# Gates of tokens 128 to 255 by indirect transfer in all expert blocks, and lo of U's second half made in two instructions

## The chip, the cores and the metric
One core of a Trainium2 chip runs the whole layer. The metric is the device time of one execution in microseconds. Before the change it was 1037.93 us, the median of three (1037.75 to 1038.24).

## What is computed
A decoder block on 256 tokens of width 1024 in float32: a token mixer (two kinds of attention, gated) and then PEER, a layer with 16384 experts. The change concerns PEER alone:

```python
def chunk_fn(xc):
    q = (xc @ wq).reshape(PEER_CHUNK, PEER_HEADS, 2, PEER_QDIM // 2)
    sc = jnp.einsum('thpd,pkd->thpk', q, subkeys)
    sv, si = lax.top_k(sc, PEER_TOPK)
    cand = sv[:, :, 0, :, None] + sv[:, :, 1, None, :]
    cv, ci = lax.top_k(cand.reshape(PEER_CHUNK, PEER_HEADS, PEER_TOPK * PEER_TOPK), PEER_TOPK)
    i1 = jnp.take_along_axis(si[:, :, 0], ci // PEER_TOPK, axis=-1)
    i2 = jnp.take_along_axis(si[:, :, 1], ci % PEER_TOPK, axis=-1)
    e = i1 * PEER_NKEYS + i2
    g = jax.nn.softmax(cv.astype(jnp.float32), axis=-1)
    act = jax.nn.gelu(jnp.einsum('td,thkd->thk', xc, u[e]))
    return jnp.einsum('thk,thkd->td', g * act, v[e])
```

Each token picks 16 experts in each of 8 heads. The kernel does not gather them: it computes gelu(x u) for all 128 blocks of 128 experts, multiplies it by a gate that is the softmax weight where an expert was picked and zero elsewhere, and multiplies by all of v.

## The kernel before
Weights come from HBM in tiles of 128x1024 through a ring of four (`raw`). Each is split so that TensorE's products are accurate: ScalarE copies it to a rounded `hi` (`loop_hi`, L1200), VectorE subtracts to get `lo` (`loop_lo`, L1676); both have three slots. TensorE then adds hi x hi, hi x lo and lo x hi.

After the token mixer (to about 270 us) come 128 **tiles of U** (`u_tile`, L831 to L833: 24 matmuls of 256 columns), whose gelu fills `big`, one block of 256 tokens per tile. Then come 128 **tiles of V** (`v_tile`, L889: 12 matmuls of 512 columns), whose stationary operands are the gated blocks, split as well: `auxh` by ScalarE (`w_hi`, L1227) and `auxl` by VectorE (`w_lo`, L1856), in three slots. TensorE's order is fixed: tile after tile.

**The router** (the choice of experts) runs beside the first 62 tiles of U: VectorE finds the best keys (`choose_keys`), GpSimd adds pairs of scores, VectorE finds the best pairs, GpSimd multiplies by key numbers and VectorE sums them, with one exponential on ScalarE. VectorE's code places `loop_lo` between these by hand: `spread(n)` makes lo of all tiles up to n+2. Head numbers 0 to 7 are those of tokens 0 to 127 and 8 to 15 those of tokens 128 to 255.

**Gates come in two ways.** A *group* (`g_group`, L844) serves four tokens and 64 blocks: ScalarE makes a one-hot `oneB` (four squares, L1215, and a Relu, L1221), VectorE a comparison `same` (L1795) and `oneA` (L1803), TensorE four matmuls of 128 columns, VectorE a reduction `gsum` (`add_parts`, L1811) and the product into `big` (`weigh`, L1818). There are 96: 64 for all tokens in blocks 0 to 63, one to a tile in U's second half, and 32 for tokens 0 to 127 in blocks 64 to 127, one to two tiles in V's first half. The gates of tokens 128 to 255 in blocks 64 to 127 are *scattered*: 128 indirect DMAs from GpSimd (L1992) add weights into the cleared `gate_d` in HBM, each sixteenth waiting for the ones before; SP brings them back as blocks of 128x128 (`gring`, four slots), and VectorE multiplies (`gate_block`, L1870), announcing each by the semaphore `gated`. That happens in V's second half.

Every engine runs its queue in order, so what stands behind a wait waits too. What sets the order around the change in V's first and second half are these lines of ScalarE's queue before:

```python
def v_step_g(i, j):
    if j % 2 == 0:
        squares_b(i, NGRP + 2 + j // 2, UNROLL // 2)
    w_hi(i, j + SPLIT - 1)
    if j % 2:
        relu_b(i, NGRP + 2 + j // 2, UNROLL // 2)
    loop_hi(i, V0 + j + SPLIT)
def v_step_gated(i, j):
    loop_hi(i, V0 + HALF + j + SPLIT)
    w_hi_gated(i, j + SPLIT)
```

Of the kernel before, what the change touches and what calls it, by code (L numbers as in the profile page):

```python
# [30 lines left out]
P = 128  # L31
D = 1024
T = 256
# [31 lines left out]
NGRP = T // 4  # L65
NGRP_V = P // 4
# [3 lines left out]
TILES_KEYS, TILES_PAIRS = 14, 25  # L70
TILES_NUMBERS = ROUTER - 2 - TILES_KEYS - TILES_PAIRS
# [20 lines left out]
def build(nc, x_d, wpre_d, u_d, v_d, par_d, cst_d, kep_d, out_d):  # L92
    with ExitStack() as ctx:
# [20 lines left out]
        eT = sb("eT", [P, 3, T])  # L114
# [187 lines left out]
        def _(sp):  # L302
# [40 lines left out]
            stream(v_d, N_PRE + NBLK, 0, HALF)  # L343
# [4 lines left out]
            sp.wait_ge(scattered, 16 * 16 * NH)  # L348

            def v_and_gates(i, j):  # L350

                sp.wait_ge(lo_done, i * UNROLL + splits(N_PRE + NBLK + HALF + GRING + j - RING + 1))
                load(splits(N_PRE + NBLK + HALF + GRING + j) % RING,
                     v_d[bass.ds(i * UNROLL + (HALF + GRING + j), 1)].rearrange("a p c -> (a p) c"))
                sp.wait_ge(S("gated"), i * UNROLL + (j + 1))
                sp.dma_start(gring[:, j % GRING, :], gate_tiles[bass.ds(i * UNROLL + (HALF + GRING + j), 1)].rearrange(
                    "a p t -> (a p) t")).then_inc(gate_in[j % GRING], 16)

            for m in range(GRING):
                sp.dma_start(gring[:, m, :], gate_tiles[HALF + m]).then_inc(gate_in[m], 16)  # L360
            for m in range(GRING):
                sp.wait_ge(lo_done, splits(N_PRE + NBLK + HALF + m - RING + 1))
                load(splits(N_PRE + NBLK + HALF + m) % RING, v_d[HALF + m])
            each_tile(sp, HALF - GRING, v_and_gates)
# [7 lines left out]
        def _(pe):  # L372
# [482 lines left out]
            for w, src in enumerate((i1f, i2f)):  # L855
                for b in range(TB):
                    m = pe.transpose(bank[6][:, w * T + b * P:w * T + (b + 1) * P], src[:, b * P:(b + 1) * P], ident)
            m.then_inc(S("keysT"), 1)
            pe.wait_ge(S("router"), 1)
            for b in range(TB):  # L860
                m = pe.transpose(bank[7][:, b * P:(b + 1) * P], chosen_w[:, b * P:(b + 1) * P], ident)
            m.then_inc(S("routerT"), 1)
# [4 lines left out]
            def g_and_u(i, j):  # L867
                g_group(i, j, UNROLL)
                u_tile(i, j, HALF)

            each_tile(pe, NGRP, g_and_u)
            g_group(0, NGRP, UNROLL)
# [35 lines left out]
            def g_and_v(i, j):  # L908
                if j % 2 == 0:
                    g_group(i, NGRP + 1 + j // 2, UNROLL // 2)  # L910
                v_tile(i, j, 1)

            v_tile(0, 0, 0, first=True, parts=1)
            each_tile(pe, 2 * NGRP_V - 4, g_and_v)
            g_group(0, NGRP + NGRP_V - 1, UNROLL // 2)
            each_tile(pe, NBLK - 3 - (2 * NGRP_V - 4), lambda i, j: v_tile(i, j, 1 + 2 * NGRP_V - 4))
# [4 lines left out]
        def _(act):  # L921
# [307 lines left out]

            def w_hi_tokens(b, tb, done):  # L1230
# [17 lines left out]
            each_tile(act, ROUTER - 2, u_step)  # L1248
            act.preload_act_table_set(LN_EXP)
            act.wait_ge(S("router_d"), 1)  # L1250
            for b in range(TB):
                of_b = gwt[:, b * P:(b + 1) * P]
                m = act.activation(of_b, of_b, ACT.Exp, scale=rs2[:, b:b + 1])
            m.then_inc(S("router_exp"), 1)
            act.preload_act_table_set(GELU)
# [15 lines left out]
            relu_b(0, NGRP, UNROLL)
            act.wait_ge(S("weighed"), 1 + NGRP)
            w_hi_tokens(0, 1, "whi_done")
            for b in range(1, SPLIT - 1):
                w_hi(0, b)
            squares_b(0, NGRP + 1, UNROLL)
            relu_b(0, NGRP + 1, UNROLL)
# [4 lines left out]
            def v_step_g(i, j):  # L1282
                if j % 2 == 0:
                    squares_b(i, NGRP + 2 + j // 2, UNROLL // 2)
                w_hi(i, j + SPLIT - 1)
                if j % 2:
                    relu_b(i, NGRP + 2 + j // 2, UNROLL // 2)
                loop_hi(i, V0 + j + SPLIT)

            def w_hi_gated(i, m):  # L1290
                act.wait_ge(S("gated"), i * UNROLL + (m + 1))
                w_hi(i, HALF + m)
# [5 lines left out]
            each_tile(act, 2 * NGRP_V - 4, v_step_g)  # L1298
            w_hi(0, HALF - 2)
# [815 lines left out]
```

## Time and profile before
| what | us |
|---|---|
| median of three | 1037.93 |
| the profiled execution | 1038.22 |
| its span, first to last instruction | 1036.3 |
| TensorE busy | 1028.7 |
| VectorE busy | 846.6 |
| ScalarE busy | 677.7 |
| GpSimd busy | 337.7 |
| U's tiles | 269 to 668 |
| V's tiles | 669 to 1033 |

Names in a row are output<-inputs. A row of a timeline gives the start in us from the span's start, the duration, engine, line, operation, and in brackets the engine's idle time before it and who ended it. Consecutive instructions overlap in the records (a start comes before the end of the one before), so the cost of one in a full queue is the distance between starts, not its duration.

### The profile page before, as it was taken

What the parts mean: (1) busy time and instruction counts of PE and PEld (TensorE: products, weight loads), DVE (VectorE), ACT (ScalarE), POOL (GpSimd) and SP (SyncE); (2) the same over time, 40 slices, a digit from 0 to 9 for tenths busy, and PEclk for the clock granted to TensorE, in tenths of its full rate; (3) what the DMA queues carried; (4) which work ended last, traced back from release to release, by engine and by line L of the source; (5) the groups of instructions that cost most, each with busy time, mean ns of one, the idle gap of its engine ahead of it and who ended that gap; (6) DMA issues with size and microseconds to landing.
All of it is one profiled execution on the core that took longest, in us unless ns stands there. A gap on an engine that the chain in (4) does not pass through costs nothing.

```text
span 1036.3 us, 21770 instructions
## 1 busy us (share of the span) xinstructions
PE 1028.7 (99%) x6945; PEld 936.3 (90%) x6945; DVE 846.6 (82%) x1673; ACT 677.7 (65%) x1283; POOL 337.7 (33%) x227
## 2 busy tenths in 40 slices
PE   8999999999999999999999999999999999999998
PEld 7798889999999999999999999988888888888887
DVE  6767886788999879999999999998888876666665
ACT  5456776665544444488988889877777764545453
POOL 0010321008102117667867688777700000000000
PEclk9999999999999999999999999999999999999999
DMA  8664555655455555566666666677755566666663
GB/s 340 250 224 154 188 181 183 196 187 187 154 191 182 180 186 182 182 171 157 161 162 157 152 158 161 143 184 183 174 174 179 182 232 207 210 222 212 220 214 123
DMA packets 80256, 194.01 MB, mean 187 GB/s; under 512 B 25296, under 2 KB 33616, under 8 KB 80208
## 3 DMA queue, kind: packets, MB, share of 16 engines
q1 hardware_dynamic: 59328, 184.79, 53.7%
q0 software_dynamic: 20736, 8.46, 7.3%
q8 instruction: 26, 0.43, 0.2%
q10 hardware_dynamic: 144, 0.14, 0.1%
q14 instruction: 22, 0.18, 0.1%
HBM read 182.81 MB, written 10.55 MB: 187 GB/s over the span
## 4 chain that ended last, share of the span: by engine, by line
PE 98%; DVE 0%; DMA 0%; ACT 0%; issue 0%; ACTq 0%; DVEq 0%
PE bank L889 33%; PE bank L831 12%; PE bank L833 12%; PE bank L832 12%; PE bank L844 4%; PE bank L385 2%; PE bank L386 2%; PE bank L387 2%; PE bank L451 2%; PE bank L771 2%; PE bank L455 1%; PE bank L467 1%; PE bank L468 1%; PE bank L469 1%; PE bank L748 1%; PE bank L749 1%
## 5 line engine op out<-in xcount | busy, mean ns | idle before, releaser
L1200 ACT ACTIVATE hi<-raw 128x1024 fp32r<-128x1024 f32 x253 | 268.2, 1060 | 248.5 <-PE bank L889 132.3
L1676 DVE TENSOR_TENSOR lo<-raw,hi 128x1024 fp32r<-128x1024 f32 x253 | 318.5, 1259 | 106.5 <-ACT hi L1200 106.2
L831 PE MATMUL bank<-xhi,hi 128*128 128x256 f32 x1024 | 292.9, 286 | 0.0
L833 PE MATMUL bank<-xhi,lo 128*128 128x256 f32 x1024 | 290.0, 283 | 0.0
L832 PE MATMUL bank<-xlo,hi 128*128 128x256 f32 x1024 | 289.7, 283 | 0.0
L1992 POOL DMA_INDIRECT gate_d<-chosen_w,chosen_at x128 | 234.9, 1835 | 72.3 <-issue 48.3
L831 PEld LDWEIGHTS bank<-xhi,hi 128*128 128x128 f32 x1024 | 196.6, 192 | 0.0
L832 PEld LDWEIGHTS bank<-xlo,hi 128*128 128x128 f32 x1024 | 196.3, 192 | 0.0
L833 PEld LDWEIGHTS bank<-xhi,lo 128*128 128x128 f32 x1024 | 196.1, 191 | 0.0
L889 PE MATMUL bank<-hi,auxh 128*128 128x512 f32 x504 | 157.4, 393 | 1.0 <-DVE auxl L1863 0.9
L889 PE MATMUL bank<-hi,auxl 128*128 128x512 f32 x504 | 155.6, 390 | 0.0
L889 PE MATMUL bank<-lo,auxh 128*128 128x512 f32 x504 | 155.5, 390 | 0.0
L1215 ACT ACTIVATE oneB<-kep,eT 128x128 fp32r<-128x128 f32 x384 | 121.5, 388 | 0.0
L889 PEld LDWEIGHTS bank<-hi,auxl 128*128 128x128 f32 x504 | 94.6, 188 | 20.0
L889 PEld LDWEIGHTS bank<-lo,auxh 128*128 128x128 f32 x504 | 94.6, 188 | 20.0
L1324 DVE TENSOR_TENSOR lo<-raw,hi 128x1024 fp32r<-128x1024 f32 x73 | 90.1, 1243 | 26.1 <-ACT hi L934 25.7
L889 PEld LDWEIGHTS bank<-hi,auxh 128*128 128x128 f32 x504 | 92.2, 188 | 18.9 <-issue 1.0
L934 ACT ACTIVATE hi<-raw 128x1024 fp32r<-128x1024 f32 x73 | 77.1, 1058 | 45.9 <-PE bank L455 19.2
L1811 DVE TENSOR_REDUCE gsum<-bank 128x256 f32<-128x512 f32 x96 | 65.8, 686 | 1.7 <-PE bank L844 0.5
L1803 DVE TENSOR_TENSOR oneA<-same,gw 128x512 fp32r<-128x512 f32 x96 | 65.7, 685 | 0.0
L1856 DVE TENSOR_TENSOR auxl<-big,auxh 128x256 fp32r<-128x256 f32 x127 | 53.3, 420 | 9.7 <-ACT auxh L1227 9.7
L1221 ACT ACTIVATE oneB<-oneB 128x512 fp32r<-128x512 f32 x96 | 59.1, 616 | 0.1
(393 smaller groups left out, 1559.6 us busy)
## 6 DMA issues: line engine op xcount, KB each, us to landing
raw<-u_d SPq DMA_DIRECT2D x128, 512.0 KB, 3.3
raw<-v_d SPq DMA_DIRECT2D x128, 512.0 KB, 3.3
raw<-wpre_d SPq DMA_DIRECT2D x70, 512.0 KB, 4.3
gate_d<-big POOLq DMA_DIRECT2D x16, 512.0 KB, 5.2
big<-wpre_d SPq DMA_DIRECT2D x8, 512.0 KB, 7.9
gring<-gate_d SPq DMA_DIRECT2D x64, 64.0 KB, 2.9
gate_d<-chosen_w,chosen_at POOLq DMA_INDIRECT x128
big<-x_d SPq DMA_DIRECT2D x4, 256.0 KB, 4.2
```

Source lines behind the costliest of these rows:

```text
L831: pe.matmul(out, wh, xhi[:, k, :], start=(k == 0), stop=False)
L832: pe.matmul(out, wh, xlo[:, k, :], start=False, stop=False)
L833: m = pe.matmul(out, wl, xhi[:, k, :], start=False, stop=(k == KT - 1))
L889: m = pe.matmul(bank[2 * b + f][:, :], a_, w_[:, s, f * 512:(f + 1) * 512], start=(first and st_ == 0), stop=False, skip_group_check=True)
L934: act.activation(hi[:, slot(n), :], raw[:, splits(n) % RING, :], ACT.Copy).then_inc(hi_done, 1)
L1200: act.activation(hi[:, slot(n), :], raw[:, splits(n) % RING, :], ACT.Copy).then_inc(hi_done, 1)
L1215: m = act.activation(oneB[:, g % 2, t, :], iota, ACT.Square, bias=i2, scale=-1.0)
L1324: dve.tensor_tensor(lo[:, slot(n), :], raw[:, splits(n) % RING, :], hi[:, slot(n), :].bitcast(F32), ALU.subtract).then_inc(lo_done, 1)
L1676: dve.tensor_tensor(lo[:, slot(n), :], raw[:, splits(n) % RING, :], hi[:, slot(n), :].bitcast(F32), ALU.subtract).then_inc(lo_done, 1)
L1803: dve.tensor_tensor(oneA[:, g % 2, :, :, :], eq_, w_.unsqueeze(3).broadcast_to([P, 4, 2, HALF]), ALU.mult).then_inc(S("oneA_ready"), 1)
L1811: dve.tensor_reduce(gsum[:, :, :], parts, AXX, ALU.add).then_inc(S("bank67_read"), 1)
L1992: pool.indirect_dma_start(gate_d, bass.IndirectOffsetOnAxis(chosen_at[:, c:c + 1], 0), chosen_w[:, P + c:P + c + 1], None, compute_op=ALU. ...
```

## The change
1. Groups serve tokens 0 to 127 only: 32 for blocks 0 to 63, one to two tiles of U's second half, and the same 32 as before in V's first half. The scattered gates now serve tokens 128 to 255 in all 128 blocks; the number of indirect DMAs stays 128.
2. Their data are needed from V's first block on. So the router treats the heads of tokens 128 to 255 first, in three pieces (heads 8 and 9, 10 to 15, then 0 to 7), with three exponentials, and GpSimd issues scatters between the sums and picks, 42 of them before the last numbers are picked.
3. In V, SP loads 128 gate blocks, VectorE multiplies each right behind lo, and ScalarE's `w_hi` waits for it.
4. In U's second half VectorE makes lo in two instructions of 512 columns.
5. SP brings `h` back behind 60 of V's steps.

```diff
-NGRP = T // 4
-NGRP_V = P // 4
+NGRP = P // 4
+GT = UNROLL // 2
+EXP_AT = (8, 20, 51)
```

SP:

```diff
-            stream(v_d, N_PRE + NBLK, 0, HALF)
+            for m in range(GRING):
+                sp.wait_ge(lo_done, splits(N_PRE + NBLK + m - RING + 1))
+                load(splits(N_PRE + NBLK + m) % RING, v_d[m])
+            sp.wait_ge(scattered, 16 * 16 * NH)
+            for m in range(GRING):
+                sp.dma_start(gring[:, m, :], gate_tiles[m]).then_inc(gate_in[m], 16)
+            def v_and_gates(i, j):
+                sp.wait_ge(lo_done, i * UNROLL + splits(N_PRE + NBLK + GRING + j - RING + 1))
+                load(splits(N_PRE + NBLK + GRING + j) % RING,
+                     v_d[bass.ds(i * UNROLL + (GRING + j), 1)].rearrange("a p c -> (a p) c"))
+                sp.wait_ge(S("gated"), i * UNROLL + (j + 1))
+                sp.dma_start(gring[:, j % GRING, :], gate_tiles[bass.ds(i * UNROLL + (GRING + j), 1)].rearrange(
+                    "a p t -> (a p) t")).then_inc(gate_in[j % GRING], 16)
+            each_tile(sp, HALF - GRING, v_and_gates)
```

TensorE, U's second half:

```diff
-                g_group(i, j, UNROLL)
+                if j % 2 == 0:
+                    g_group(i, j // 2, GT)
                 u_tile(i, j, HALF)
```

ScalarE:

```diff
+            def weights_exp(z, b, c0, c1):
+                act.preload_act_table_set(LN_EXP)
+                act.wait_ge(S("router_d"), z + 1)
+                of_heads = gwt[:, c0 * 16:c1 * 16]
+                act.activation(of_heads, of_heads, ACT.Exp, scale=rs2[:, b:b + 1]).then_inc(S("router_exp"), 1)
+                act.preload_act_table_set(GELU)
+            u_steps(0, EXP_AT[0])
+            weights_exp(0, 1, NH, NH + 2)
+            u_steps(EXP_AT[0], EXP_AT[1])
+            weights_exp(1, 1, NH + 2, 2 * NH)
...
+            act.wait_ge(S("weighed"), 1 + NGRP)
             w_hi_tokens(0, 0, "whi_tokens")
+            act.wait_ge(S("gated"), 1)
             w_hi_tokens(0, 1, "whi_done")
+            w_hi_gated(0, 1)
...
             def v_step_g(i, j):
                 if j % 2 == 0:
+                    squares_b(i, NGRP + 2 + j // 2, GT)
-                w_hi(i, j + SPLIT - 1)
+                w_hi_gated(i, j + SPLIT - 1)
                 if j % 2:
+                    relu_b(i, NGRP + 2 + j // 2, GT)
                 loop_hi(i, V0 + j + SPLIT)
-            def v_step_gated(i, j):
-                loop_hi(i, V0 + HALF + j + SPLIT)
-                w_hi_gated(i, j + SPLIT)
+            def v_step(i, j):
+                w_hi_gated(i, HALF + j)
+                loop_hi(i, V0 + HALF + j + 1)
```

VectorE:

```diff
+            numbers(NH, NH + 2, 6, 9)
+            weights(0, NH, NH + 2)
+            dve.wait_ge(S("cleared"), 16 * 16)
+            addresses(NH, NH + 2)
+            for z in range(3):
+                choose_pairs(NH + 2 + 2 * z, 12 + 3 * z)
+            from_best(NH + 2, 2 * NH)
+            numbers(NH + 2, 2 * NH, 18, 26)
...
+            def loop_lo_halves(i, n):
+                dve.wait_ge(hi_done, i * UNROLL + splits(n + 1))
+                dve.tensor_tensor(lo[:, slot(n), 0:512], raw[:, splits(n) % RING, 0:512],
+                                  hi[:, slot(n), 0:512].bitcast(F32), ALU.subtract).then_inc(S("lo_first"), 1)
+                dve.tensor_tensor(lo[:, slot(n), 512:1024], raw[:, splits(n) % RING, 512:1024],
+                                  hi[:, slot(n), 512:1024].bitcast(F32), ALU.subtract).then_inc(lo_done, 1)
...
+            w_lo_tokens(0, 0, "whi_tokens", 1, "wlo_tokens")
+            add_parts(0, NGRP, GT)
+            keys_equal(0, NGRP + 3, GT)
+            gate_block(0, 0)
+            gate_block(0, 1)
+            w_lo_tokens(0, 1, "whi_done", 1, "wlo_done")
+            gate_block(0, 2)
+            w_lo(0, 1)
...
+            def v_step(i, j):
+                w_lo(i, j + SPLIT - 1)
+                loop_lo(i, V0 + j + SPLIT)
+                gate_block(i, j + SPLIT)
             def v_step_g(i, j, keys=True, rows=True):
...
                 loop_lo(i, V0 + j + SPLIT)
+                gate_block(i, j + SPLIT)
```

The order of the instructions shows three places. ScalarE, one odd step of the loop over V's first half (`auxh` is w_hi, `oneB` the Relu, ISA computes an address), before:

```order
L1227 ISA
L1227 ACTIVATE auxh<-big 128x256
L1220 REGISTER_ALU
L1221 ACTIVATE oneB<-oneB 128x512 [waits dist_sq]
L1199 REGISTER_ALU [waits tile_loaded2]
L1200 ACTIVATE hi<-raw 128x1024 [waits tile_used]
```

and now:

```order
L1229 REGISTER_ALU
L1224 ISA [waits gated]
L1224 ACTIVATE auxh<-big 128x256
L1217 REGISTER_ALU
L1218 ACTIVATE oneB<-oneB 128x512 [waits dist_sq]
L1196 REGISTER_ALU [waits tile_loaded2]
L1197 ACTIVATE hi<-raw 128x1024 [waits tile_used]
```

The copy to `auxh` has got a wait for `gated`, on the register operation ahead of it, and hi stands behind both.

VectorE, the same loop (`auxl` is w_lo, `oneA` the group's operand), an odd step, before:

```order
L1856 ISA [waits whi_done]
L1856 TENSOR_TENSOR auxl<-big,auxh 128x256
L1816 REGISTER_ALU
L1818 ISA [waits bank67_read]
L1818 TENSOR_TENSOR big<-gsum,big 128x64x4
L1803 ISA [waits same]
L1803 TENSOR_TENSOR oneA<-same,gw 128x512
L1675 REGISTER_ALU
L1676 TENSOR_TENSOR lo<-raw,hi 128x1024 [waits hi_done]
```

and now:

```order
L1916 ISA [waits whi_done]
L1916 TENSOR_TENSOR auxl<-big,auxh 128x256
L1865 REGISTER_ALU
L1867 ISA [waits bank67_read]
L1867 TENSOR_TENSOR big<-gsum,big 128x64x4
L1852 ISA [waits same]
L1852 TENSOR_TENSOR oneA<-same,gw 128x512
L1681 REGISTER_ALU
L1682 TENSOR_TENSOR lo<-raw,hi 128x1024 [waits hi_done]
L1928 REGISTER_ALU
L1930 ISA [waits gate_in0]
L1930 TENSOR_TENSOR big<-big,gring 128x128
```

The product with `gring`, which announces `gated`, stands last in the step, behind lo.

GpSimd, the router and the scatters (L2026 sums of pairs, L2036 picks), before:

```order
L1975 TENSOR_TENSOR big<-big 128x256 [waits keys_chosen]
L1975 TENSOR_TENSOR big<-big 128x256 x3
L1975 TENSOR_TENSOR big<-big 128x256 [waits pairs_chosen] x12
L1983 TENSOR_TENSOR big<-big 128x256 [waits placed] x32
L1992 DMA gate_d<-chosen_w,chosen_at 2097152x1 [waits chosen,router]
L1992 DMA gate_d<-chosen_w,chosen_at 2097152x1 x15
L1992 DMA gate_d<-chosen_w,chosen_at 2097152x1 [waits scattered]
```

and now:

```order
L2036 TENSOR_TENSOR big<-big 128x256 [waits placed] x4
L2046 DMA gate_d<-chosen_w,chosen_at 2097152x1 [waits chosen,router,keys_chosen]
L2046 DMA gate_d<-chosen_w,chosen_at 2097152x1 x2
L2026 TENSOR_TENSOR big<-big 128x256 [waits pairs_chosen] x2
L2046 DMA gate_d<-chosen_w,chosen_at 2097152x1 x8
L2036 TENSOR_TENSOR big<-big 128x256 [waits placed] x4
L2046 DMA gate_d<-chosen_w,chosen_at 2097152x1
L2036 TENSOR_TENSOR big<-big 128x256 [waits placed] x4
L2046 DMA gate_d<-chosen_w,chosen_at 2097152x1
L2036 TENSOR_TENSOR big<-big 128x256 [waits placed] x4
L2046 DMA gate_d<-chosen_w,chosen_at 2097152x1
L2046 DMA gate_d<-chosen_w,chosen_at 2097152x1 [waits chosen,router]
```

The scatters have moved from behind all sums and picks to between them; the list goes on in this manner.

## Rows read from the trace of the kernel before
**Rows 1.** The page: span, and busy time, share and instructions of each engine (part 1).
```profile
span 1036.3 us, 21770 instructions
...
PE 1028.7 (99%) x6945; PEld 936.3 (90%) x6945; DVE 846.6 (82%) x1673; ACT 677.7 (65%) x1283; POOL 337.7 (33%) x227
```

**Rows 2.** The chain of waits in time: start us, us, what.
```profile
491.96 0.39 PE bank L844 x4
...
495.29 0.39 PE bank L844 x4
...
708.18 5.53 PE bank L889 x24
...
714.11 5.53 PE bank L889 x24
...
858.75 168.96 PE bank L889 x744
...
1027.70 5.45 PE bank L904 x24
```

**Rows 3.** Timeline of ScalarE in U's first half: start us, us, instruction [idle before].
```profile
437.36 1.06 ACT L1200 ACTIVATE hi<-raw 128x1024 fp32r<-128x1024 f32 x1 [1.82 <-PE bank L833]
...
440.24 1.06 ACT L1200 ACTIVATE hi<-raw 128x1024 fp32r<-128x1024 f32 x1 [1.34 <-PE bank L833]
```

**Rows 4.** Timeline of TensorE between tiles 61 and 62 of U: the transposes.
```profile
448.69 0.60 PE L857 MATMUL bank<-kep,big 128*128 128x128 f32 x4
```

**Rows 5.** Timeline of VectorE in V's first half.
```profile
737.41 0.42 DVE L1856 TENSOR_TENSOR auxl<-big,auxh 128x256 fp32r<-128x256 f32 x1 [0.36 <-ACT auxh L1227]
737.85 0.69 DVE L1811 TENSOR_REDUCE gsum<-bank 128x256 f32<-128x512 f32 x1
738.46 0.42 DVE L1795 TENSOR_TENSOR same<-kep,eT 128x256 f32<-128x256 f32 x1
738.79 1.22 DVE L1676 TENSOR_TENSOR lo<-raw,hi 128x1024 fp32r<-128x1024 f32 x1
```

**Rows 6.** Timeline of ScalarE and VectorE in V's second half.
```profile
899.90 1.06 ACT L1200 ACTIVATE hi<-raw 128x1024 fp32r<-128x1024 f32 x1 [1.35 <-PE bank L889]
...
901.00 1.23 DVE L1676 TENSOR_TENSOR lo<-raw,hi 128x1024 fp32r<-128x1024 f32 x1 [0.95 <-ACT hi L1200]
902.14 0.28 DVE L1870 TENSOR_TENSOR big<-big,gring 128x128 f32 x1
```

**Rows 7.** Timeline of both late in V's first half, VectorE's addresses constant.
```profile
831.69 0.40 ACT L1227 ACTIVATE auxh<-big 128x256 fp32r x1
...
832.13 0.43 DVE L1856 TENSOR_TENSOR auxl<-big,auxh 128x256 fp32r<-128x256 f32 x1 [0.25 <-ACT auxh L1227]
```

**Rows 8.** Timeline of ScalarE at the step of rows 5.
```profile
736.87 0.40 ACT L1227 ACTIVATE auxh<-big 128x256 fp32r x1
...
738.42 0.40 ACT L1227 ACTIVATE auxh<-big 128x256 fp32r x1
738.73 0.62 ACT L1221 ACTIVATE oneB<-oneB 128x512 fp32r<-128x512 f32 x1
```

**Rows 9.** Timeline of ScalarE and VectorE in U's first half: the router.
```profile
444.69 1.28 ACT L1249 ACT_TABLE_LOAD   x1
...
445.36 1.39 DVE L1756 TENSOR_REDUCE big<-big 128x16 f32<-128x256 f32 x4
...
313.47 0.75 DVE L1690 MAX8 big<-big 128x8 f32<-128x256 f32 x2
...
316.36 1.21 DVE L1676 TENSOR_TENSOR lo<-raw,hi 128x1024 fp32r<-128x1024 f32 x1
```

**Rows 10.** Instructions on gate_d (ns min/median/max, first and last start), timelines of GpSimd and VectorE.
```profile
L1992 POOL DMA_INDIRECT gate_d<-chosen_w,chosen_at x128: 1553/1572/3488, 450.5 to 749.5; - x128
...
542.95 2.60 POOL L1992 DMA_INDIRECT gate_d<-chosen_w,chosen_at  x1 [0.30 <-issue]
...
542.89 1.22 DVE L1676 TENSOR_TENSOR lo<-raw,hi 128x1024 fp32r<-128x1024 f32 x1 [0.23 <-ACT hi L1200]
```

More of the change, by code:

```diff
@@ L347, in _ @@
                 sp.dma_start(h[:, b, :], out_d[b * P:(b + 1) * P, :]).then_inc(S("h_back"), 16)
[L348 to L364, printed above, removed]
+            each_tile(sp, HALF, lambda i, j: v_and_gates(i, HALF - GRING + j))
             for z, (b, c, w) in enumerate(out_parts_v):
@@ L855, in _ @@
             for w, src in enumerate((i1f, i2f)):
-                for b in range(TB):
-                    m = pe.transpose(bank[6][:, w * T + b * P:w * T + (b + 1) * P], src[:, b * P:(b + 1) * P], ident)
+                m = pe.transpose(bank[6][:, w * P:(w + 1) * P], src[:, 0:P], ident)
             m.then_inc(S("keysT"), 1)
[L859 to L862, printed above, removed]
+            pe.wait_ge(S("router"), 3)
+            pe.transpose(bank[7][:, 0:P], chosen_w[:, 0:P], ident).then_inc(S("routerT"), 1)
             for j in range(ROUTER, HALF):
@@ L1228, in w_hi, with w_hi_gated @@
                                ACT.Copy).then_inc(S("whi_done"), 1)
+            def w_hi_gated(i, b):
+                act.wait_ge(S("gated"), i * UNROLL + (b + 1))
+                w_hi(i, b)
             def w_hi_tokens(b, tb, done):
@@ new lines, in weights, with addresses @@
+            def weights(z, c0, c1):
+                sums, ones = smx[:, c0:c1], smx[:, 16 + c0:16 + c1]
+                dve.wait_ge(S("router_exp"), z + 1)
+                link(dve.tensor_reduce(sums, g3[:, c0:c1], AXX, ALU.add))
+                link(dve.reciprocal(ones, sums))
+                dve.tensor_tensor(w3[:, c0:c1], g3[:, c0:c1], ones.unsqueeze(2).broadcast_to([P, c1 - c0, 16]),
+                                  ALU.mult).then_inc(S("router"), 1)
+            def addresses(c0, c1):
+                of_heads = slice(c0 * 16, c1 * 16)
+                link(dve.scalar_tensor_tensor(caf[:, of_heads], i1f[:, of_heads], 128.0, i2f[:, of_heads], ALU.mult, ALU.add))
+                dve.tensor_scalar(chosen_at[:, c0 * 16 - P:c1 * 16 - P], caf[:, of_heads], float(P), tok_at,
+                                  ALU.mult, ALU.add).then_inc(S("chosen"), 1)
@@ L1782, in _ @@
+            from_best(NH + 2, 2 * NH)
+            numbers(NH + 2, 2 * NH, 18, 26)
+            weights(1, NH + 2, 2 * NH)
+            addresses(NH + 2, 2 * NH)
+            for c in range(1, NH):
+                choose_keys(c)
+                spread(26 + (11 * c) // 7)
+            keys_ready()
+            for z in range(4):
+                choose_pairs(2 * z, 40 + 3 * z)
+            from_best(0, NH)
+            numbers(0, NH, 49, ROUTER - 2)
+            weights(2, 0, NH)
             dve.wait_ge(S("keysT"), 1)
-            dve.tensor_copy(eT[:, 0:2, :], bank[6][:, :].rearrange("p (w t) -> p w t", w=2)).then_inc(S("bank67_read"), 1)
+            dve.tensor_copy(eT[:, 0:2, :], bank[6][:, 0:2 * P].rearrange("p (w t) -> p w t", w=2)).then_inc(S("bank67_read"), 1)
@@ L1976, in _, with pick @@
                                    ALU.add).then_inc(S("pair_sums"), 1)
-            for c in range(16):
+            def pick(c):
+                q = (c - NH) % (2 * NH)
                 for side in range(2):
-                    pool.wait_ge(S("placed"), 2 * c + side + 1)
+                    pool.wait_ge(S("placed"), 2 * q + side + 1)
                     e3 = eqt[c % 2][side].rearrange("p (k a) -> p k a", k=16)
```

305 lines of the change are left out of this document (155 added, 150 removed).

## The prediction
> **What bounds the kernel now.** I read the page first, then the chain of waits, then the timeline of single engines. The span is 1036.3 us and TensorE is busy for 99% of it, VectorE 82%, ScalarE 65% [rows 1]; the granted clock is full in every stretch. The chain that ended last is TensorE from end to end in both large stages [rows 2]. Its pieces give the prices. In U's second half a group of gate matmuls plus a tile of U takes 495.29 - 491.96 = 3.33, of which a tile alone is 2.88, the spacing of ScalarE's hi instructions in U's first half [rows 3]; so a group costs 0.44 there. In V's first half two blocks and a group take 714.11 - 708.18 = 5.93. In V's second half 62 blocks take 168.96, 2.725 each. The last two blocks take 5.45. So whatever takes a group from TensorE is worth its time, as long as ScalarE and VectorE still deliver one block's four operands (hi, lo of V; auxh, auxl of the gated activations) every 2.965 us in V's first half and every 2.725 in its second.
>
> **Removed.** 32 of 96 groups, all in U's second half: 32 x 0.44 = -14.1 us. Three of six transposes, at most 0.60 / 4 each [rows 4]: -0.4. The squares, Relus, comparisons and reductions of 32 groups leave ScalarE and VectorE too, which are not on the path there, so nothing more comes off.
>
> **Lo in halves.** Two instructions of 512 columns at a spacing of 0.61 [rows 5] (738.46 - 737.85) take 1.22 where one takes 1.14 (902.14 - 901.00) [rows 6]: +0.08 each on VectorE, 63 times. Two tiles of U and a group now last 2 x 2.88 + 0.44 = 6.2 us, in which VectorE has 4 x 0.61 of lo and four group instructions (0.61, 0.33, 0.33, 0.61): 4.3. Hidden by 1.9 us of idle time; without that cover it would be 5 us.
>
> **V: a wait that closes a ring.** This is the term that decides. In step j of V's first half ScalarE now does w_hi of block j+2 behind the wait for `gated` (block j+2), and hi of V's tile j+3 stands behind it in ScalarE's queue. The gating of block j+2 is VectorE's last instruction of step j-1, behind lo of tile j+2, which waits for ScalarE's hi of tile j+2. So hi(n), lo(n), gate(n), w_hi(n), hi(n+1) are one chain, each the start of the next, with no slack to gain on. Before, tokens 128 to 255 of the first half needed no gating, and in the second half gates ran ahead (four in the ring, gate j+3 done behind lo of j+2), so that the same chain spanned two blocks. One turn, from rows:
> - hi start to lo start: 901.00 - 899.90 = 1.10 [rows 6];
> - lo to gate: 1.14; the gate lasts 0.28 [rows 6];
> - gate end to w_hi start: 0.04 where the address is a constant (831.69 + 0.40 to 832.13) [rows 7], 0.14 where it is computed from the loop's register (736.87 + 0.40 to 737.41) [rows 5, 8]. Those rows are VectorE's behind ScalarE; the new wait stands on the register operation itself, as there, so I take 0.14, with 0.04 as the other end;
> - w_hi to the next start on ScalarE: 0.31 (738.73 - 738.42) [rows 8].
>
> Sum 2.97, taken as 2.96, against TensorE's 2.725: V's second half loses 63 x 0.235 = **+14.8**. With the constant's 0.04 it would be 2.86 and +8.5.
>
> In V's first half more stands in the ring. Even steps (the four squares stand ahead of the wait and are done before it ends): after w_hi (0.40 + 0.14) VectorE does auxl (0.33), the reduction (0.61), the comparison (0.33) and then lo (1.14), gate (0.28), 0.14: 3.37. (A start follows an instruction of 0.41 after 0.33 [rows 5].) Odd steps: w_hi 0.31, Relu 0.62 less the 0.09 by which its follower starts early, hi to lo 1.10, then 1.14 + 0.28 + 0.14: 3.50. A pair is 6.84 with rounding against TensorE's 5.93. 28 pairs: **+25.5**. Six last steps have less in them: +1.2. At the start TensorE has about 1.1 us in hand (estimate: auxl of block 2 is due that long before its tile): -1.1. At the end the last two blocks are interleaved; auxl of block 127 comes 2.96 after that of 126 where TensorE needs 5.45 / 8 = 0.68 between them: +2.3. The passage from U to V itself: the halves of block 0 now wait for the last weighing and for the first gate; nearly as long as before (-0.4). The ring in all: **+42.3**; with 0.04 for all latencies of 0.14 some 150 of them give back 0.1 each, +27.
>
> **U's first half.** The router is now done in three pieces, and VectorE waits for GpSimd where that has scatters in its queue ahead of sums and picks. GpSimd's 128 indirect transfers move from behind everything to between these: 42 are in U's first half, and all 16-packs wait for completion. Tile 12 is the place that I can price. Tiles start at 448.69 - 2.88 x (62 - j), tile 12 at 304.7. ScalarE does hi of tile 11 only behind the exponential and two table loads of 1.28 [rows 9]: some 1.6 late, so lo of tile 11 ends at 300.1. Before lo of tile 12 VectorE has four picks' sums (1.39) [rows 9], five small instructions for weights and addresses (estimate 1.6), and eight instructions on pairs (316.36 - 313.47 = 2.9) [rows 9]: lo starts at 306.0 and ends 1.2 later, 2.5 us late. Three more joints with GpSimd (the numbers of heads 10 to 15, the first pair sums of tokens 0 to 127, the last numbers) come out within 2 us of their due time; I give them 1 us together. **+3.5**, between 0 and 9.
>
> **Scatters.** 86 are left when the last numbers are picked, near 453. Before, their spacing was (749.5 - 450.5) / 127 = 2.35 [rows 10], waits for a pack among it. At that pace they start until 453 + 85 x 2.35 = 653, land some 4.5 later, and the gates' loads (2.9 to landing, 0.4 to issue) would be in at 661, where block 0 wants its gate at about 658. So cover ends just there. But a scatter that starts just behind a lo of 1024 columns takes 2.60 in place of the median 1.57 [rows 10], 1.03 more; with 512 columns less is to be waited for. The sum takes 2.2, done before 650, cost 0; ends are 0 and +6. The Trainium skill says in SBUF — State Buffer, "SBUF: two separate sides", that VectorE with two SBUF inputs and a reading GpSimd hold a shared pair for a whole instruction, whoever starts first. By that rule a half holds it for about half as long, and the scatters are in time; the row of 2.60 agrees, while no run here shows the halves.
>
> SP's queue has the loads of V's tiles 0 to 3 ahead of the wait for `scattered`, and each gate load behind its V load: the ring gives each over 11 us for 2.9. The reload of h (moved behind 60 blocks) has 180 us. Both nothing.
>
> **Sum.** -14.1 - 0.4 + 42.3 + 3.5 = +31.3, on the profiled span of 1036.3: 1067.6. That execution took 1038.22, 1.92 above its span, and 0.29 above the median of 1037.93. So 1069.2, say **1069**.
>
> **Rivals.**
> - The ring turns at constant-address latency (0.04) everywhere: +27 - 14.5 + 3.5 = +16, 1054; without a slip in U 1050. For: ScalarE's register operation may be shorter than VectorE's. Against: the one row of a computed address behind a wait. 18%.
> - The scatters are late: +6 more, 1075, if their spacing stays at 2.35. Against: halves and a less busy VectorE. 10%.
> - Faster, the other side: the ring does not bind and TensorE keeps its 2.725 and 5.93. Then only -14.5 and the slip count: 1023 to 1027. It needs mean turns under 2.93 us where 2.96 and 3.43 come out of rows (mean 3.2), each link being one that another pair of engines must wait for. The order of the instructions leaves no way around it; it decides from a mean of 0.08 us per block up (10 us over 125 blocks). 8%: 5 of them clearly faster, 2 within the noise, 1 slower.
> - The change does less than it says: no; the groups are gone from TensorE's order, 14.1 us at 0.44.
>
> The main case has 64%. Faster by over 0.2% (what a measurement here can tell from no change) 0.05, within it 0.02, slower 0.93. Range: 1050 (no late address, no slip) to 1080 (slip of 9, late scatters).
>
> **What would show it.** In V's second half hi's spacing should be 2.96 (2.86 in the rival), with ScalarE idle before w_hi until VectorE's gate, not before hi until TensorE; VectorE idle until ScalarE's hi; TensorE idle in each block by 0.2, waiting for auxl. In V's first half pairs of 6.84. In U's second half groups every 6.2. A first gate load before 652. I am wrong if hi in V still waits for TensorE.

## The result and the profile after

The change is slower: 1070.74 us, the median of four (1070.33 to 1072.60), against 1038.09 (1037.75 to 1038.68) before; ratio 1.0317, 95% interval 1.0300 to 1.0335. The forecast was 1069, in a range of 1050 to 1080. The profiled execution took 1070.51 us with a span of 1068.7, where the prediction's sum gave 1067.6. One of gate_first's four executions below took 1419.68 us at a mean granted clock of 0.655; it is left out of every number.

The page of the kernel after: span, busy times, and the shares of the chain that ended last, by engine and by line.

```profile
span 1068.7 us, 21198 instructions
...
PE 1046.5 (98%) x6814; PEld 913.6 (85%) x6814; DVE 817.6 (76%) x1694; ACT 629.7 (59%) x1128; POOL 327.6 (31%) x227
...
PE 57%; DVE 15%; issue 14%; ACT 11%; DVEq 1%; ACTq 1%; DMA 0%; SPq 0%
```

The engines' busy shares hardly differ from [rows 1], and "PE 98%" would let one take TensorE for the bound still. The chain says otherwise: only 57% of it is TensorE's, where it was 98% before. TensorE's busy time has even grown by 18 us with 131 instructions fewer. The ends of matmuls are modelled, and in V one that is followed by a short pause counts as longer (the hi x auxh matmuls last 414 ns in the mean where they lasted 393 before). So the chain and the idle times decide here, not the busy share. Idle time by who ended it, in the kernel after (engine, output, line; who was waited for; us in total, times, longest):

```profile
ACT auxh L1224 <- DVE big L1930: 175.5, 125, 2.0
DVE auxl L1916 <- ACT auxh L1224: 83.8, 126, 0.7
PEld bank L886 <- DVE auxl L1916: 33.4, 87, 0.5
PE bank L830 <- DVE lo L1682: 2.8, 3, 1.9
PE bank L901 <- DVE auxl L1916: 1.9, 1, 1.9
```

ScalarE waits 125 times in V for the gate product (L1930), and no longer once before hi for TensorE, as it did in [rows 6]. TensorE's weight loads wait for auxl: it is now the engine that is fed late.

**The ring in V's second half.** Timelines of ScalarE and VectorE, kernel after (start us, us, instruction, idle before it):

```profile
952.20 1.04 ACT L1197 ACTIVATE hi<-raw 128x1024 fp32r<-128x1024 f32 x1
954.82 0.42 ACT L1224 ACTIVATE auxh<-big 128x256 fp32r x1 [1.58 <-DVE big L1930]
955.15 1.04 ACT L1197 ACTIVATE hi<-raw 128x1024 fp32r<-128x1024 f32 x1
```

```profile
953.27 1.23 DVE L1682 TENSOR_TENSOR lo<-raw,hi 128x1024 fp32r<-128x1024 f32 x1 [0.41 <-ACT hi L1197]
954.41 0.28 DVE L1930 TENSOR_TENSOR big<-big,gring 128x128 f32 x1
```

One can follow the turn: hi at 952.20, lo 1.07 later, the gate 1.14 behind lo, auxh 0.41 behind the gate's start (0.28 of it, then 0.13 until ScalarE goes on), the next hi 0.33 later: 2.95 from hi to hi. TensorE needs 2.725 for a block [rows 2].

**The ring in V's first half**, VectorE in the kernel after. Two steps last from lo to lo 732.32 - 725.46 = 6.86, where TensorE could do them in 5.93:

```profile
725.46 1.22 DVE L1682 TENSOR_TENSOR lo<-raw,hi 128x1024 fp32r<-128x1024 f32 x1
726.59 0.28 DVE L1930 TENSOR_TENSOR big<-big,gring 128x128 f32 x1
727.56 0.42 DVE L1916 TENSOR_TENSOR auxl<-big,auxh 128x256 fp32r<-128x256 f32 x1 [0.68 <-ACT auxh L1224]
...
732.32 1.22 DVE L1682 TENSOR_TENSOR lo<-raw,hi 128x1024 fp32r<-128x1024 f32 x1
```

**U's first half.** TensorE's matmul that opens tile 12 (timeline, kernel after), and VectorE's piece before it:

```profile
306.81 0.36 PE L830 MATMUL bank<-xhi,hi 128*128 128x256 f32 x1 [1.89 <-DVE lo L1682]
...
356.49 0.35 PE L830 MATMUL bank<-xhi,hi 128*128 128x256 f32 x1 [0.49 <-DVE lo L1682]
359.96 0.36 PE L830 MATMUL bank<-xhi,hi 128*128 128x256 f32 x1 [0.37 <-DVE lo L1682]
```

```profile
299.09 1.22 DVE L1682 TENSOR_TENSOR lo<-raw,hi 128x1024 fp32r<-128x1024 f32 x1 [2.18 <-ACT hi L1197]
300.23 1.39 DVE L1760 TENSOR_REDUCE big<-big 128x16 f32<-128x256 f32 x4
...
305.45 2.35 DVE L1682 TENSOR_TENSOR lo<-raw,hi 128x1024 fp32r<-128x1024 f32 x2
```

Between the lo of tile 11 at 299.09 and that of tile 12 at 305.45 lie 6.4 us, in which TensorE has work for 2.88. The transposes that were at 448.69 [rows 4] are at 452.19: a slip of 3.5. In this trace V's first group of gate matmuls starts at 656.67, where the kernel before had it at 667.76.

**Scatters and gate loads**, all transfers on gate_d of the kernel after from 449 to 647 us (ns min/median/max, first and last start), and SP's first four loads of gates:

```profile
L2046 POOL DMA_INDIRECT gate_d<-chosen_w,chosen_at x87: 1561/1640/2387, 448.9 to 646.6; - x87
```

```profile
L347 SPq DMA_DIRECT2D gring<-gate_d x4: 328/432/433, 651.4 to 652.7; - x4
```

Their spacing is (646.6 - 448.9) / 86 = 2.30. The last one starts at 646.6, the loads leave from 651.4, and block 0 of V begins at 657.7 after 0.5 us of waiting: in time.

**The tail.** The chain's last entries, and windows of the kernel after (window, length, then busy time of PE, PEld, DVE, ACT, POOL with instructions, the granted clock of TensorE, DMA share, GB/s):

```profile
1056.41 1.23 DVE lo L1682
1058.89 6.67 PE bank L901 x21
```

```profile
1057.00:1060.00 3.00, 1.11 (x5) 0.97 (x6) 1.33 (x4) 0.42 (x1) 0.00 (x0) 1.00 0.02 5
1060.00:1064.00 4.00, 4.00 (x13) 3.09 (x12) 1.31 (x2) 0.00 (x0) 0.00 (x0) 0.57 0.28 105
1064.00:1068.00 4.00, 1.54 (x7) 0.94 (x5) 1.37 (x2) 0.00 (x0) 0.00 (x0) 1.00 0.42 159
```

21 matmuls take 6.67 us where before 24 took 5.45 [rows 2]. TensorE had stood for 1.9 us; from 1060.1 to 1063.8 nine matmuls then start 0.41 apart on average in place of 0.23, at a granted clock of 0.57 of full speed, that is mostly at the lower level of 1.2 GHz. That costs 1.6 us which no step of the prediction had.

### The profile page after: what moved, and what is told of

Same layout as the page of the kernel before. It is cut to its first block, busy times and chain, and to the rows that moved or that the text cites. A ratio compares the mean times of both kernels' runs of the same rounds, so it can differ in the third digit from the quotient of the medians.

```text
span 1068.7 us, 21198 instructions
## 1 busy us (share of the span) xinstructions
PE 1046.5 (98%) x6814; PEld 913.6 (85%) x6814; DVE 817.6 (76%) x1694; ACT 629.7 (59%) x1128; POOL 327.6 (31%) x227
## 4 chain that ended last, share of the span: by engine, by line
PE 57%; DVE 15%; issue 14%; ACT 11%; DVEq 1%; ACTq 1%; DMA 0%; SPq 0%
PE bank L830 10%; PE bank L832 10%; PE bank L831 10%; ACT hi L1197 8%; DVE lo L1682 6%; DVE big L1930 3%; ACT auxh L1224 3%; PE bank L384 2%; PE bank L385 2%; PE bank L386 2%; PE bank L450 2%; PE bank L770 2%; DVE gsum L1860 2%; DVE oneA L1852 2%; PE bank L454 1%
## 5 line engine op out<-in xcount | busy, mean ns | idle before, releaser
L830 PE MATMUL bank<-xhi,hi 128*128 128x256 f32 x1024 | 291.7, 285 | 2.8 <-DVE lo L1682 2.8
L1682 DVE TENSOR_TENSOR lo<-raw,hi 128x1024 fp32r<-128x1024 f32 x190 | 242.4, 1280 | 38.3 <-ACT hi L1197 37.6
L2046 POOL DMA_INDIRECT gate_d<-chosen_w,chosen_at x128 | 231.3, 1807 | 74.0 <-issue 48.1
L886 PE MATMUL bank<-hi,auxh 128*128 128x512 f32 x504 | 168.0, 414 | 1.8 <-DVE auxl L1923 0.5
L1224 ACT ACTIVATE auxh<-big 128x256 fp32r (+1 forms) x127 | 53.1, 418 | 175.5 <-DVE big L1930 175.5
L886 PEld LDWEIGHTS bank<-hi,auxh 128*128 128x128 f32 x504 | 85.1, 188 | 46.7 <-DVE auxl L1916 33.4
L1330 DVE TENSOR_TENSOR lo<-raw,hi 128x1024 fp32r<-128x1024 f32 x73 | 90.1, 1244 | 26.1 <-ACT hi L931 25.9
L1889 DVE TENSOR_TENSOR lo<-raw,hi 128x512 fp32r<-128x512 f32 x63 | 43.6, 693 | 54.9 <-ACT hi L1197 54.9
L1212 ACT ACTIVATE oneB<-kep,eT 128x128 fp32r<-128x128 f32 x256 | 81.1, 389 | 0.0
L384 PE MATMUL bank<-xhi,hi 128*128 128x256 f32 x192 | 56.2, 293 | 0.0
```

The source lines that it names most:

```text
L384: pe.matmul(out, wh, xh, start=(k == 0), stop=False)
L830: pe.matmul(out, wh, xhi[:, k, :], start=(k == 0), stop=False)
L886: m = pe.matmul(bank[2 * b + f][:, :], a_, w_[:, s, f * 512:(f + 1) * 512], start=(first and st_ == 0), stop=False, skip_group_check=True)
L1212: m = act.activation(oneB[:, g % 2, t, :], iota, ACT.Square, bias=i2, scale=-1.0)
L1224: act.activation(auxh[:, s * T:(s + 1) * T], big[:, bass.ds(i * (UNROLL * T) + b * T, T)], ACT.Copy).then_inc(S("whi_done"), 1)
L1330: dve.tensor_tensor(lo[:, slot(n), :], raw[:, splits(n) % RING, :], hi[:, slot(n), :].bitcast(F32), ALU.subtract).then_inc(lo_done, 1)
```

## The experiments

The theory: the gate product behind lo closes a ring of ScalarE and VectorE, and that is worth +42.3; the rest of the change is worth -14.5 and +3.5. The main rivals: the loss comes from the added work or transfers in V, or from the scatters. All ratios are against the kernel before, run on the same chip (its medians were 1038.07 to 1038.46). The sizes of single parts below are read from the profiled executions; V is counted from its first group of gate matmuls on.

**gate_first.** The product stands ahead of lo, in both of VectorE's loops in V. The same instructions, in another order:

```diff
                 w_lo(i, j + SPLIT - 1)
-                loop_lo(i, V0 + j + SPLIT)
                 gate_block(i, j + SPLIT)
+                loop_lo(i, V0 + j + SPLIT)
...
-                loop_lo(i, V0 + j + SPLIT)
                 gate_block(i, j + SPLIT)
+                loop_lo(i, V0 + j + SPLIT)
```

> In both V steps the gating of block j+3 is moved ahead of lo of tile j+3 on VectorE; the instructions and their number stay. Ring theory: hi, lo, gate, w_hi no longer follow each other in one turn; what is left of it (w_hi, auxl, group work, gate) is 0.54 + 0.33 + 0.94 + 0.28 + 0.14 = 2.2 us, under TensorE's 2.965 and 2.725. So pairs of 5.93 in V's first half, 2.725 a block in its second, and about 43 us off 1070.7: 1027 to 1029, hi in V waiting for TensorE again. Rival, VectorE or the gate loads simply have too much to do in V (128 gatings and loads in place of 64): the order changes nothing, 1068 to 1072.

Measured: 1026.80 us, the median of three (1026.79, 1026.80, 1029.31), ratio 0.990 (0.988 to 0.992); the profiled execution took 1026.80, span 1025.0. So 43.7 us hang on the place of an instruction of 0.28 us, 1.6 of them through the clock in the tail. The chain of this kernel in V is TensorE's again:

```profile
839.51 176.88 PE bank L886 x780
1016.39 5.45 PE bank L901 x24
```

and ScalarE in V's second half waits for TensorE before hi, with 2.71 between them:

```profile
899.47 1.06 ACT L1197 ACTIVATE hi<-raw 128x1024 fp32r<-128x1024 f32 x1 [1.35 <-PE bank L886]
...
902.18 1.06 ACT L1197 ACTIVATE hi<-raw 128x1024 fp32r<-128x1024 f32 x1 [1.35 <-PE bank L886]
```

All of the added products, gate loads and waits are still there. They cost nothing off the ring.

**ring_dose.** V's lo in halves as well, with the change's order: a dose of some 0.07 us in a link of the ring, and on VectorE.

```diff
 in v_step and v_step_g:
-                loop_lo(i, V0 + j + SPLIT)
+                loop_lo_halves(i, V0 + j + SPLIT)
```

> As the change, but lo of V is made in two instructions of 512 columns too, which puts the gate 1.20 to 1.22 us behind lo's start in place of 1.14. Ring theory: each of some 125 turns is 0.06 to 0.08 longer, 1070.7 + 7.5 to 10 = 1078 to 1081; spacing of hi in V's second half 3.01 to 3.03 in place of 2.95. If the wait were for something outside this ring (gate loads, TensorE), nothing: 1070 to 1072.

Measured: 1079.61 (two executions), ratio 1.0397 (1.0376 to 1.0417), 8.9 above the change. VectorE in V's second half, where lo starts 3.03 apart:

```profile
949.31 0.69 DVE L1889 TENSOR_TENSOR lo<-raw,hi 128x512 fp32r<-128x512 f32 x1 [0.41 <-ACT hi L1197]
...
950.52 0.28 DVE L1930 TENSOR_TENSOR big<-big,gring 128x128 f32 x1
...
952.34 0.69 DVE L1889 TENSOR_TENSOR lo<-raw,hi 128x512 fp32r<-128x512 f32 x1 [0.40 <-ACT hi L1197]
```

The two traces also differ by the clock, and not only by the dose. This one has a stretch at the lower clock in U (0.72 and 0.71 from 306 to 312, against 1.00 in the change), and V's first group starts at 658.83, 2.2 later; its tail has the full clock, 1.6 less (21 matmuls in 5.06 us). From V's first group to these 21 matmuls it is 1069.41 - 658.83 = 410.6 us here and 1058.89 - 656.67 = 402.2 in the change: the dose itself costs 8.4, 0.07 for each of some 125 blocks.

**gate_first_dose.** Both edits together: the same dose, off the ring.

> The gate ahead of lo, and V's lo in halves. Ring theory: lo is in no ring, VectorE has 5.2 + 0.14 of 5.93 us in a pair, so the same as with the gate first alone, 1027 to 1030. If VectorE's load is the bound, 7 to 10 us more than with the gate first alone.

Measured: 1027.68 (1026.51 and 1028.84), ratio 0.9897 (0.9877 to 0.9916). V takes 1024.7 - 656.6 = 368.1 us of its trace, and 1025.0 - 656.9 = 368.1 of gate_first's. The same work that costs 8.4 us in the ring costs nothing outside of it. VectorE's load is no bound.

**gate_first_v2.** The order is changed in V's second half alone (`v_step`), which splits the ring's price.

> The gate ahead of lo only in the steps of V's second half; the first half keeps the change's order. Ring theory, by its two terms: 63 x (2.95 - 2.725) = 14 and the tail's 2 come back, the first half's 26 to 27 stay: 1070.7 - 16 = 1054 to 1055.5, with pairs of 6.86 in the first half and 2.725 in the second.

Measured: 1052.87 (1052.55 and 1053.18), ratio 1.0139 (1.0119 to 1.0159), about 1 below the expectation. The span of the profiled execution is 1051.4, 17.3 below that of the change. Its tail, at the full clock and without the wait, has the length of before again:

```profile
873.85 168.93 PE bank L886 x744
1042.78 5.46 PE bank L901 x24
```

The tail begins at 1042.78 and V's first group at 657.30, against 1056.03 and 656.67 in the change. So the 63 turns of the second half are worth (1056.03 - 656.67) - (1042.78 - 657.30) = 13.9, and were priced at 14.8. The tail is worth 4.0 more, 2.1 of wait and 1.6 of clock among it; the expectation had 2 for it, since I had not counted the clock, and so lay too high. What remains above gate_first is the first half's: V takes 394.1 us here and 368.1 there, 26.0, priced at 25.5 + 1.2 - 1.1 = 25.6 (the -0.4 of the passage from U to V is in both kernels). The pairs of the first half last 6.86 here too.

**ring_const.** ScalarE's loop over V's second half is written out, so that the operation behind `gated` has a constant address. Nothing else changes.

```diff
-            each_tile(act, HALF - 1, v_step)
+            for j in range(HALF - 1):
+                v_step(0, j)
```

> The change with ScalarE's loop over V's second half written out, so that w_hi's address is a constant; VectorE and the order stay. If the wait on a register operation costs 0.08 to 0.10 more than one on the copy itself, hi's spacing in the second half falls from 2.95 to 2.85 to 2.87: 60 x 0.08 to 0.10 = 5 to 6 less, 1064.5 to 1066. If the latency has nothing to do with the address: 1070 to 1071.

Measured: 1065.47 (1063.28 and 1067.66), ratio 1.026 (1.0233 to 1.0288). The median lies in the expected range only because it is the mean of two times outside it, 4.4 apart, so the trace has to decide. ScalarE in this kernel:

```profile
952.31 1.04 ACT L1197 ACTIVATE hi<-raw 128x1024 fp32r<-128x1024 f32 x1
954.85 0.42 ACT L1224 ACTIVATE auxh<-big 128x256 fp32r<-128x256 f32 x1 [1.49 <-DVE big L1931]
955.17 1.04 ACT L1197 ACTIVATE hi<-raw 128x1024 fp32r<-128x1024 f32 x1
```

The turn is 2.86 in place of 2.95, and the wait 1.49 in place of 1.58: the computed address costs 0.09 behind a wait. 63 x 0.09 = 5.7. The 21 last matmuls start at 1053.12, 5.8 earlier than in the change. The rest of the profiled execution's gain (1070.51 - 1063.28 = 7.2) is the clock: it is full in the tail of this trace. The execution of 1067.66 has a mean clock of 0.998 where the traced one has 1.000; where it lost its 4.4 us, no trace shows.

**lo_whole.** The change, with lo of U's second half in one instruction again.

```diff
-                    loop_lo_halves(i, N_PRE + HALF + j + SPLIT)
+                    loop_lo(i, N_PRE + HALF + j + SPLIT)
```

> As the change, but lo of U's second half is one instruction of 1024 columns again. My term for the scatters: their spacing goes back from 2.30 to about 2.38 with durations of 2.6 among them, the last starts near 653.6 in place of 646.6, and block 0's gate comes about 3 us late (the loads' issue and landing behind it): 1073 to 1075. If halves matter for nothing else than that and the cover is longer than I think: 1070 to 1071.

Measured: 1073.29 (1073.19, 1073.39), ratio 1.0336 (1.0315 to 1.0356). It met the expectation of scatters that come 2.5 us late, for another reason. Its last scatter does start late, at 653.3, but VectorE's first gate product (661.25) stands right behind the comparison before it, with no idle time, and from V's first group (659.55) to the 21 last matmuls (1061.59) it is 402.0 us, as in the change. The loss is in U: the transposes between tiles 61 and 62 are already at 454.82, 2.6 us behind those of the change, and up to there the two kernels have the same instructions. The next runs separate the two.

**gate_first_whole.** gate_first with the same edit, **gate_first_again** the same file as gate_first, both on one chip.

> The gate first, lo of U's second half whole. Scatters' term: with the ring gone the late first gate still costs the 2.5 us that it cost with the ring in place (1073.3 against 1070.7), since TensorE is the bound behind it: 1029 to 1030 against 1026.8. If V had room to catch up, less: 1027 to 1028.

> The gate first once more, beside the other two: 1026.5 to 1028.

Measured: whole 1027.68 (1026.47 to 1029.60), ratio 0.9903 (0.9886 to 0.9920); again 1028.89 (1026.47 to 1029.29), ratio 0.9903 (0.9886 to 0.9919). Again lies above its expected range, and the expected cost of a whole lo is not there, although its last scatter starts 3.5 us later than gate_first's 646.9:

```profile
L2046 POOL DMA_INDIRECT gate_d<-chosen_w,chosen_at x128: 1548/1641/3698, 303.3 to 650.4; - x128
```

Both spread over the same two values. The windows behind the stall at tile 12, gate_first_again (span 1027.0) and then gate_first_whole (span 1024.7), columns as above:

```profile
306.00:309.00 3.00, 2.47 (x15) 2.50 (x16) 3.00 (x7) 0.27 (x1) 2.96 (x1) 0.72 0.40 149
309.00:312.00 3.00, 3.00 (x20) 3.00 (x20) 3.00 (x13) 0.77 (x1) 2.74 (x3) 0.71 0.97 284
```

```profile
306.00:309.00 3.00, 2.46 (x20) 2.49 (x21) 3.00 (x7) 0.29 (x1) 2.97 (x1) 1.00 0.48 171
309.00:312.00 3.00, 3.00 (x27) 3.00 (x26) 3.00 (x13) 1.06 (x1) 2.73 (x3) 1.00 0.96 257
```

Both had the stall of 1.9 us (1.90 and 1.89); one of them ran some 3.4 us at the lower clock behind it. lo_whole's trace has that stretch as well, at 0.74 and 0.69 in the same windows, and the profiled execution of the change at 1.00 in both. That is lo_whole's +2.6 (its second execution, 1073.39, has the same mean clock, 0.997, but no trace).

**before_halves.** The kernel before, with lo in halves in U's second half.

> The kernel before with lo of U's second half in two instructions and nothing else. VectorE has 0.23 us of idle time in 3.32 and gets 0.06 to 0.08 more to do: the same time, 1037.5 to 1038.7. The scatters that meet this stretch (86 of 128) get closer, 2.30 or less in place of 2.38, with no durations of 2.6 among them, without effect on the time. If the fixed cost of an instruction were larger than I take it, U's steps would be longer than 3.32 and the time up by some us.

Measured: 1038.25 (ten executions, 1037.73 to 1038.90), ratio 1.000 (0.999 to 1.0009). The halves cost TensorE nothing, even with a group per tile. The scatters in its trace end at 731.1 in place of 749.5 [rows 10], and of those that start until 655 none takes over 2.23 us, where 20 of the kernel before take over 2.5.

**gate_first_spreads.** gate_first, with lo of the next tiles placed earlier in VectorE's router, at the two joints where TensorE had waited.

```diff
             weights(0, NH, NH + 2)
+            spread(10)
...
             weights(1, NH + 2, 2 * NH)
+            spread(27)
             addresses(NH + 2, 2 * NH)
```

> The gate ahead of lo, and lo of one more tile placed right behind the weights of heads 8 and 9 (before their addresses and the next pairs) and behind those of heads 10 to 15. The stalls of 1.9, 0.5 and 0.4 us that the change's trace has in U's first half are for lo behind that work, so all go if the place is the cause: 2.8 less than the gate first alone, 1024 to 1026. If GpSimd's lateness is the cause, the stalls move to the next tile and the time stays at 1027 to 1028.

Measured: 1025.57 (1025.52 to 1025.64), ratio 0.9876 (0.9860 to 0.9893). The wait at tile 12 is gone, but the second lo did not take the other joint's away as expected. It moved and grew: a stall of 1.66 us at 358.74.

```profile
358.74 0.36 PE L830 MATMUL bank<-xhi,hi 128*128 128x256 f32 x1 [1.66 <-DVE lo L1682]
```

**gate_first_even.** The same, with one more lo ahead in the loop behind it.

```diff
-                spread(26 + (11 * c) // 7)
+                spread(28 if c == 1 else 26 + (11 * c) // 7)
```

> As the version with the gate first and the two early los, and lo of one further tile behind the choice of the keys of head 1, where two choices of 2.35 us had come to stand between two los and TensorE waited 1.7 us once. If the place alone is the cause, that wait goes: 1023.6 to 1024.4. If VectorE has no time left there, it comes back at a later tile, 1025 to 1026.

Measured: 1024.79 (1024.75 to 1025.13), ratio 0.9870 (0.9854 to 0.9887). It lies between the two expectations: the wait of 1.66 is gone, but 0.76 us of waits for lo are left at 363.34 and 366.82. The four executions lie within 0.4 us. This version beats both kernels: 13.3 us below the one before on the same chip.

**even_whole.** gate_first_even, with the whole lo in U's second half.

> The version with the gates ahead of lo and the three early lo's in the router, with lo of U's second half in one instruction again. Theory: the whole lo costs nothing; the 2.5 us by which the change with a whole lo was longer came from a stretch of 3.5 us at a granted clock of 0.7 behind the stall at tile 12, which this version doesn't have. The last scatter then starts near 646 to 649, and the four first gate loads leave before 653, with the first gate wanted near 656. 1024.5 to 1025.4 us, beside 1024.79 with halves. Rival (the halves are worth what they seemed to be, through scatters that end earlier): 1026.5 to 1027.5 us, with TensorE idle before block 0 of V until VectorE's gate.

Measured: 1025.09 (1024.70, 1025.04, 1025.13 and 1026.73), ratio 0.9873 (0.9856 to 0.9889). No cost. The one of 1026.73, the profiled one, has its lower clock in the first 20 us, in the token mixer. Its scatters take 340.6 us from first to last start:

```profile
L2048 POOL DMA_INDIRECT gate_d<-chosen_w,chosen_at x128: 1547/1642/3744, 306.2 to 646.8; - x128
```

and gate_first_even's 337.5:

```profile
L2048 POOL DMA_INDIRECT gate_d<-chosen_w,chosen_at x128: 1547/1643/3735, 304.4 to 641.9; - x128
```

The halves bring the scatters in 3.1 us earlier, in front of a need that is later still.

## Why the prediction was right, point by point

**The ring, +42.3: right.** A turn came out of rows as 2.96 and was 2.95 measured, a pair as 6.84 and was 6.86. The two steps of a pair were priced at 3.37 and 3.50, which is 6.87 and not 6.84; over 28 pairs that slip is 0.8 us. The second half's share was 13.9 of the 14.8 it was given, the first half's 26.0 of 25.6, and the passage from U to V gave back its 0.4. U ends where the sum put it (V's first group at 656.7 against 656.8), so V takes 412.0 of the span against 410.8. That is 43.5 more than before (1036.3 - 667.8 = 368.5); without the 1.6 of clock in the tail it is 41.9, against 42.3. Two experiments show the cause: gate_first takes the ring away and 43.7 us with it, and ring_dose against gate_first_dose shows the same 0.07 us per block costing 8.4 us inside and nothing outside.

**The computed address: the taken value was right.** 0.14 stood against 0.04, with 18% on the rival. ring_const measured the difference as 0.09 per turn, in V's second half; in the first half and on VectorE no run took the computed address away.

**The tail, +2.3: one part was missing.** The wait there was nearly as predicted, 1058.89 - 1056.57 less a spacing of 0.23 = 2.1. Behind it the clock fell, for 1.6 us. The step "auxl of block 127 comes 2.96 after that of 126" priced the wait alone. This is most of the 1.1 us by which the span exceeds the sum.

**Groups and transposes, -14.5: right.** gate_first, without the ring, has a span of 1025.0; 1036.3 - 14.1 - 0.4 + 3.5 = 1025.3.

**U's first half, +3.5: the sum was right, its parts were not.** The slip to tile 62 is exactly 3.5, but of 1.9 at tile 12 (2.5 predicted: the five small instructions took 0.9 instead of 1.6, while lo of tile 11 ended at 300.3, where 300.1 was taken), 0.9 at tiles 29 and 30 (1 predicted for three joints), and restarts behind them. The agreement of the sum is partly luck. The range's upper end here should have named the clock: gate_first's executions and those of its variants with a mean clock of 0.998 are 2.3 to 3.1 longer than the others.

**Scatters, 0: right.** A spacing of 2.2 was taken, which would end them at 640; it was 2.30 and they ended at 646.6, still before 650. By the rule of the Trainium skill, SBUF — State Buffer, "SBUF: two separate sides", a half holds the shared pair for a shorter time, and the traces agree in this direction: no scatter of the last 87 took over 2.39, where one had taken 2.60 [rows 10]. By the same rule a lo that starts inside a scatter would have to wait for it, and there the trace of the kernel before disagrees: its lo took 1.23 as ever.

```profile
539.22 1.56 POOL L1992 DMA_INDIRECT gate_d<-chosen_w,chosen_at  x1 [0.30 <-issue]
...
539.58 1.23 DVE L1676 TENSOR_TENSOR lo<-raw,hi 128x1024 fp32r<-128x1024 f32 x1 [0.23 <-ACT hi L1200]
```

The halves are worth nothing here all the same. With a whole lo the scatters of gate_first_whole end at 650.4, and VectorE's first gate product follows at 658.35 without waiting. The case that the prediction priced at +6, an end at 653 with U no later, occurs in no run, so that price stays untested. My later expectation that a whole lo costs 2.5 us was wrong, though lo_whole's time seemed to confirm it.

**The rival of the other side** (the ring does not bind, 1023 to 1027) had the right price: gate_first is that kernel. Its statement "the order of the instructions leaves no way around it" holds for the change's order, and one swapped pair is the way around.

## What to carry to other kernels

Where engines with queues in order feed each other, follow one operand round: if step n+1 of one engine waits for the last instruction of another's step n, the kernel runs at the sum of that circle, whatever the busy shares say; put the short instruction that releases someone ahead of the long one that nobody waits for so soon. Add such a circle up from starts in the trace, idle links included, before changing the order, and treat a gain of 14 us in one stage as nothing until that sum is below the bound of every other stage. When two kernels differ by 2 to 3 us, look where in the span the difference arises, and at the granted clock there, before a run that met its expectation is taken as proof.

## What was not expected of the hardware

**A stall of 1.9 us can cost more than itself.** Behind it the granted clock may fall to the lower of its two levels, 1.2 GHz, for some 3.4 us. TensorE in gate_first_again, where matmuls start 0.12 apart until 307.31 and then 0.21:

```profile
306.53 0.36 PE L830 MATMUL bank<-xhi,hi 128*128 128x256 f32 x1 [1.90 <-DVE lo L1682]
...
307.31 0.38 PE L830 MATMUL bank<-xhi,hi 128*128 128x256 f32 x1
307.49 0.41 PE L831 MATMUL bank<-xlo,hi 128*128 128x256 f32 x1
307.70 0.41 PE L832 MATMUL bank<-xhi,lo 128*128 128x256 f32 x1
...
310.69 0.32 PE L831 MATMUL bank<-xlo,hi 128*128 128x256 f32 x1
```

That is 1.5 us. In addition TensorE then waits 1.26 us at 358.50 for ScalarE's hi; in traces without the stretch it waits 0.49 to 0.51 for lo at that tile. It does not happen each time: nine traces have the stall of 1.9 us at tile 12, and three of them the lower clock behind it (gate_first_again, ring_dose, lo_whole). Four have the stall of 1.9 to 2.0 us in the tail, and two of them the lower clock there (the change and lo_whole).

Gate_first, its dose, whole and again have 13 executions: six at 1026.5 to 1026.8 with a mean clock of 1.000, seven at 1028.8 to 1029.6 with 0.998. Kernels without that stall (the one before, before_halves, gate_first_spreads, gate_first_even, even_whole) have 56 executions with a clock on record, and only four of them 0.998: three of the kernel before, at 1039.67 to 1039.87, and the one of even_whole that was low in the token mixer. So such a stretch is far more frequent with the stall, and it also occurs without it. What decides is open; gate_first_spreads, with a stall of 1.66 us, has its four executions within 0.12 us of each other. A mean clock of 0.998 does not say where the stretch was: the change's trace has it in the tail, ring_dose's in U. The one execution of the change at 1072.60 has 0.997, as lo_whole's with both stretches. It probably had both too, but no trace of it shows that.

**A register-computed address behind a wait costs 0.09 to 0.10 us more than a constant one**: 0.09 on ScalarE by ring_const, 0.10 on VectorE by the rows of the kernel before [rows 5, 7, 8]. In the ring that was 5.7 us for 63 turns.
